# Dilated scores of a two-layer decoder: high and low parts in place of plain fp32, two heads in the two row halves

## The reference, cut to what matters

```python
cq, ck, cv, rq, rk, rv, rg = jnp.split(h @ w_in, cuts, axis=-1)
q = rotary(cq, pos, ROPE_DIM, ROPE_THETA); k = rotary(ck, pos, ROPE_DIM, ROPE_THETA)
scores = jnp.einsum('brnqhd,brnkhd->brnhqk', qs, kk) * (dh ** -0.5)   # per window and dilation
p = jnp.exp(scores - m)                                               # softmax per row
```

## Time and profile before

| | before |
|---|---|
| median of 3 runs | 1432.67 us (1432.28 to 1432.73) |
| profiled execution, its own time | 1432.46 us |
| its span in the trace | 1430.7 us |
| PE busy | 1420.2 us, 99% |
| DVE / ACT / POOL busy | 728.8 / 532.8 / 107.5 us |
| granted TensorE clock | 0.998 of full speed |
| PE's share of the chain that ended last | 96% |

### The profile page before, as it was taken

The page is one execution under the profiler, slowest core; times in us unless marked ns, Lnnn a source line. Parts: engine busy times, 40 slices in busy tenths (PEclk is TensorE's granted clock), DMA queues, the critical chain, the costliest instruction groups (busy, mean ns, idle before and its releaser), DMA issues.

```text
span 1430.7 us, 17936 instructions
## 1 busy us (share of the span) xinstructions
PE 1420.2 (99%) x6780; PEld 1181.7 (83%) x6780; DVE 728.8 (51%) x1025; ACT 532.8 (37%) x809; POOL 107.5 (8%) x90
## 2 busy tenths in 40 slices
PE   9999999999999999999999999999999999999998
PEld 8888888888888888888877788988888888888887
DVE  6656655454444443334567755765544444443332
ACT  5632544332323222322645634543433222322221
POOL 0012200200000000100201111100020000000010
PEclk9999999999999999999999999999999999999999
DMA  8721321232232333333321112541133232233321
GB/s 333 259 88 60 118 74 45 90 101 91 100 102 89 103 100 107 103 104 133 99 78 53 66 45 75 191 141 65 59 103 103 89 102 91 100 101 104 99 78 60
DMA packets 41514, 146.73 MB, mean 103 GB/s; under 512 B 4976, under 2 KB 5104, under 8 KB 41456
## 3 DMA queue, kind: packets, MB, share of 16 engines
q1 hardware_dynamic: 38288, 138.17, 28.9%
q10 hardware_dynamic: 3168, 7.74, 1.5%
HBM read 143.79 MB, written 2.10 MB: 102 GB/s over the span
## 4 chain that ended last, share of the span: by engine, by line
PE 96%; DVE 1%; ACT 1%; issue 1%; DMA 0%; SPq 0%; POOLq 0%; POOL 0%; ACTq 0%
PE acc L1436 28%; PE acc L1438 28%; PE acc L1437 28%; PE acc L1484 3%; PE acc L1486 3%; PE acc L1485 3%; PE aux L1779 1%; PE acc L1803 1%; PE aux L1791 1%; DMA raw<-in_weights 0%; PE aux L1438 0%; PE aux L1437 0%; PE aux L1436 0%; DVE xpt_lo L1143 0%; DVE xp L1160 0%
## 5 line engine op out<-in xcount | busy, mean ns | idle before, releaser
L879 DVE TENSOR_TENSOR w_lo<-raw,w_hi 128x1024 fp32r<-128x1024 f32 x255 | 314.7, 1235 | 328.5 <-ACT w_hi L444 328.4
L1436 PE MATMUL acc<-u_hi,w_hi 128*128 128x512 f32 x1056 | 413.0, 391 | 0.0
L1438 PE MATMUL acc<-u_hi,w_lo 128*128 128x512 f32 x1056 | 411.1, 389 | 0.0
L1437 PE MATMUL acc<-u_lo,w_hi 128*128 128x512 f32 x1056 | 410.9, 389 | 0.0
L444 ACT ACTIVATE w_hi<-raw 128x1024 fp32r<-128x1024 f32 x255 | 268.1, 1052 | 375.9 <-DVE tmp L1235 192.2
L1436 PEld LDWEIGHTS acc<-u_hi,w_hi 128*128 128x128 f32 x1056 | 198.3, 188 | 42.4 <-issue 2.3
L1438 PEld LDWEIGHTS acc<-u_hi,w_lo 128*128 128x128 f32 x1056 | 198.2, 188 | 41.7
L1437 PEld LDWEIGHTS acc<-u_lo,w_hi 128*128 128x128 f32 x1056 | 198.3, 188 | 40.4
L1436 PE MATMUL acc<-act_hi,w_hi 128*128 128x512 f32 (+1 forms) x374 | 141.6, 379 | 0.0
L1438 PE MATMUL acc<-act_hi,w_lo 128*128 128x512 f32 (+1 forms) x374 | 140.9, 377 | 0.0
L1437 PE MATMUL acc<-act_lo,w_hi 128*128 128x512 f32 (+1 forms) x374 | 140.8, 377 | 0.0
(11 more groups left out here) (195 smaller groups left out, 1598.1 us busy)
## 6 DMA issues: line engine op xcount, KB each, us to landing
raw<-in_weights SPq DMA_DIRECT2D x255, 512.0 KB, 3.5
hT<-in_x_t ACTq DMA_DIRECT2D x4, 512.0 KB, 6.4
x_tok<-in_x ACTq DMA_DIRECT2D x4, 512.0 KB, 6.8
out_h<-y_tok SPq DMA_DIRECT2D x4, 512.0 KB, 2.7
mem_tok<-in_mem SPq DMA_DIRECT2D x1, 1024.0 KB, 9.1
memT<-in_mem_t SPq DMA_DIRECT2D x3, 256.0 KB, 5.3
raw<-in_weights SPq DMA_DIRECT2D x2, 256.0 KB, 4.6
cs_d<-in_cs_d ACTq DMA_DIRECT2D x1, 512.0 KB, 3.5
```

The costliest lines, as they stand in the source:

```text
L879: dve.tensor_tensor(w_lo[:, s, :], raw[:, s, :], w_hi[:, s, :].bitcast(F32), ALU.subtract)\
L1436: pe.matmul(out, w_h, x_h, start=first, stop=False)
L1437: pe.matmul(out, w_h, x_l, start=False, stop=False)
L1438: return pe.matmul(out, w_l, x_h, start=False, stop=last)
```

## The change

Rotated q and k of the dilated heads go to a ring of three tiles (`turned_d`). ScalarE rounds each to fp32r (`dil_hi_part`) and VectorE subtracts (`dil_lo_part`). The scores become three matmuls of these parts for each block of rows, and each of the three is issued for the one head and then for the other. A block of `scores` is now rows (0, 1) or (2, 3) of both heads, where it was all rows of one head. `rotate` and `partners` of the dilated tiles stand one unit further back. In the loop over pairs VectorE's `masked`, `maxima` and `normalise` are spread differently.

```diff
-        tq_d = at("tq_d", 8, [P, 4, S])
-        tk_d = at("tk_d", 24, [P, 4, S])
+        tq_hi = at("tq_hi", 8, [P, 4, S], F32R)
+        tq_lo = at("tq_lo", 0, [P, 4, S], F32R)
+        tk_hi = at("tk_hi", 24, [P, 4, S], F32R)
+        tk_lo = at("tk_lo", 16, [P, 4, S], F32R)
+        turned_d = at("turned_d", 82, [P, 3, S])
...
+        def rot_tile(r):
+            return turned_d[:, r % 3, :] if r < 8 else tq[:, r - 8, :]
+        def dil_parts(r):
+            return (tq_hi, tq_lo) if r < 4 else (tk_hi, tk_lo)
+        def ds_tile(p, i, e):
+            return aux_at["ds", p] + 2 * i + e
...
+                def dil_hi_part(r):
+                    act.wait_ge(rot_ready, r + 1)
+                    act.activation(dil_parts(r)[0][:, r % 4, :], turned_d[:, r % 3, :], ACT.Copy).then_inc(dhi_ready, 1)
...
-                    partners(j, a0 + B_QK + j, 32)
+                    if j:
+                        partners(j - 1, a0 + B_QK + j - 1, 32)
+                    if j >= 3:
+                        dil_hi_part(j - 3)
                 for n in range(4):
                     split(u0 + U_RV + n + LEAD)
+                    if n == 0:
+                        partners(7, a0 + B_QK + 7, 32)
+                        dil_hi_part(5)
+                    if n == 1:
+                        dil_hi_part(6)
+                        dil_hi_part(7)
                     if n in (1, 2):
                         exps(n - 1)
...
                 def rotate(r):
-                    dst = (tq_d if r < 4 else tk_d)[:, r % 4, :] if r < 8 else tq[:, r - 8, :]
+                    dst = rot_tile(r)
+                    if 3 <= r < 8:
+                        dve.wait_ge(dlo_ready, r - 2)
                     cs = cs_d if r < 8 else cs_r
                     dve.tensor_tensor(dst, tmp[:, r % 2, :], cs[:, 0, :], ALU.mult)
                     dve.wait_ge(shifted, r + 1)
                     dve.tensor_tensor(tmp[:, 2 + r % 2, :], tmp[:, 2 + r % 2, :], cs[:, 1, :], ALU.mult)\
                         .then_inc(rot_half, 1)
-                def masked(p, heads):
-                    for e in heads:
-                        for i in range(TT):
+                def dil_lo_part(r):
+                    dve.wait_ge(dhi_ready, r + 1)
+                    hi, lo = dil_parts(r)
+                    dve.tensor_tensor(lo[:, r % 4, :], turned_d[:, r % 3, :], hi[:, r % 4, :].bitcast(F32), ALU.subtract)\
+                        .then_inc(dlo_ready, 1)
+                def masked(p, rows):
+                    for i in rows:
+                        for e in range(2):
                             o, w = ROWS[i]
-                            t = aux_at["ds", p] + 4 * e + i
+                            t = ds_tile(p, i, e)
                             dve.wait_ge(aux_done, t + 1)
                             dve.scalar_tensor_tensor(out=dp[:, e, o:o + w], in0=auxs[t % 4][:, 0:w],
                                                      scalar=float(DH) ** -0.5, in1=band[:, S - w:S], op0=ALU.mult,
                                                      op1=ALU.add).then_inc(aux_free_v, 1)
+                def maxima(p, e):
...
                     if j >= 2:
+                        rotate(j - 2)
                         dve.wait_ge(rot_half, j - 1)
                     scaled(a0 + B_QK + j, tmp[:, j % 2, :])
-                    if j:
-                        rotate(j - 1)
+                    if j >= 4:
+                        dil_lo_part(j - 4)
                 for n in range(4):
                     split(u0 + U_RV + n + LEAD)
                     if n == 0:
+                        dil_lo_part(4)
+                        rotate(6)
+                    if n == 1:
                         rotate(7)
-                    if n == 1:
+                        dil_lo_part(5)
                         dve.wait_ge(rot_half, 8)
-                        masked(0, (0, 1))
-                        maxima(0)
+                        masked(0, range(TT))
+                        maxima(0, 0)
+                        maxima(0, 1)
                     if n >= 2:
+                        dil_lo_part(4 + n)
                         normalise(n - 2)
...
                     side(first)
                     if p + 1 < DIL_H // 2:
-                        masked(p + 1, (0,))
+                        masked(p + 1, (0, 1))
                     side_rotate(first)
+                    if p + 1 < DIL_H // 2:
+                        masked(p + 1, (2, 3))
+                        maxima(p + 1, 0)
                     y_lo_part(p, acc(t)[:, :], PHM1 + p + 1, acc_drained)
                     if p + 1 < DIL_H // 2:
-                        masked(p + 1, (1,))
-                        maxima(p + 1)
+                        maxima(p + 1, 1)
                     side(second)
+                    if p + 1 < DIL_H // 2:
+                        normalise(2 * p + 2)
                     side_rotate(second)
                     if p + 1 < DIL_H // 2:
-                        normalise(2 * p + 2)
                         normalise(2 * p + 3)
...
-                def scores(p, e):
-                    pe.wait_ge(rot_ready, 5 + p)
-                    q = slice(DH * e, DH * (e + 1))
-                    for i in range(TT):
-                        t = aux_at["ds", p] + 4 * e + i
-                        aux_free(pe, t)
-                        pe.matmul(auxs[t % 4][:, 0:(i + 1) * P], tq_d[q, p, i * P:(i + 1) * P],
-                                  tk_d[q, p, 0:(i + 1) * P], start=True, stop=True).then_inc(aux_done, 1)
+                def scores(p, rows):
+                    pe.wait_ge(dlo_ready, 5 + p)
+                    for i in rows:
+                        tok, keys = slice(i * P, (i + 1) * P), slice(0, (i + 1) * P)
+                        outs = [auxs[ds_tile(p, i, e) % 4][:, keys] for e in range(2)]
+                        q = [slice(DH * e, DH * (e + 1)) for e in range(2)]
+                        for e in range(2):
+                            aux_free(pe, ds_tile(p, i, e))
+                        for e in range(2):
+                            pe.matmul(outs[e], tq_hi[q[e], p, tok], tk_hi[q[e], p, keys], start=True, stop=False)
+                        for e in range(2):
+                            pe.matmul(outs[e], tq_lo[q[e], p, tok], tk_hi[q[e], p, keys], start=False, stop=False)
+                        for e in range(2):
+                            pe.matmul(outs[e], tq_hi[q[e], p, tok], tk_lo[q[e], p, keys], start=False, stop=True)\
+                                .then_inc(aux_done, 1)
...
-                           after=lambda q: scores(0, q) if q < 2 else None)
+                           after=lambda q: scores(0, (2 * q, 2 * q + 1)) if q < 2 else None)
...
-                        scores(p + 1, 0)
+                        scores(p + 1, (0, 1))
                     values(p)
                     if p + 1 < DIL_H // 2:
-                        scores(p + 1, 1)
+                        scores(p + 1, (2, 3))
```

More of the change, by code:

```diff
@@ L303, in program @@
         rot_ready = sem("rot_ready")
+        dhi_ready = sem("dhi_ready")
+        dlo_ready = sem("dlo_ready")
         dve_step = sem("dve_step")
@@ L1266, in masked @@
                                                      op1=ALU.add).then_inc(aux_free_v, 1)
-                def maxima(p):
-                    for e in range(2):
-                        for i in range(TT):
[L1272 to L1275, removed]
+                def maxima(p, e):
+                    for i in range(TT):
+                        o, w = ROWS[i]
+                        dve.wait_ge(aux_free_v, freed_v(ds_tile(p, i, e)))
+                        dve.tensor_reduce(nmax[:, e, i:i + 1], dp[:, e, o:o + w], AX.X, ALU.max,
+                                          negate=True).then_inc(max_ready, 1)
                 def normalise(h):
```

## The result

The changed kernel takes 1424.32 us (median of four runs, 1424.19 to 1424.54) where the kernel before took 1432.55 beside it: a ratio of 0.9942 (0.993 to 0.9954), 8.2 us or 0.57% faster. The forecast was 1424.7. The profiled execution took 1424.38 us with a span of 1422.6.

What follows compares the result with a forecast made beforehand. TensorE bounds the kernel, busy 1420.2 of 1430.7 us. Streams save 9.5 us, less waits of 0.4 and 1.2, so 7.9 off 1432.46 gives 1424.6, plus 0.2 for the median: 1424.7 us, range 1422.8 to 1430.9.

Steps and rivals of the forecast that it cites:

- The streams: TensorE's score blocks: each of four pairs of heads falls from 4.26 to 1.88 us, 9.5 us saved.
- 1.88, 2.64 and 3.76 us for a pair: TensorE's score matmuls per pair: halves side by side 1.88 (taken), weight loads queueing 2.64, single file 3.76 us.
- 128 columns: Score matmuls of 128 columns in fp32r: 0.109 us each, taken from the transposes; upper bound 0.21, costing 1.2 us more.
- The first block's new wait: First score block waits for tile 4's low part, expected 2.2 us ahead of TensorE: no wait.
- Behind the retention values: After head 0's transposes, TensorE waits once for VectorE's drain of the retention values to free an acc tile: 0.4 us.
- At the transposes of heads 3 and 5: TensorE waits for an aux tile at the transitions to pairs 1 and 2: 0.6 us more each, 1.2 together.
- The sum: Whole kernel: 9.5 less 0.4 less 1.2 gives 7.9 us saved, forecast 1424.7 us.
- (a): Rival on score blocks: weight loads of the two halves queue, a pair takes 2.64 us, 1427.4 us; chance 0.17.
- (b): Rival on score blocks: the halves run in single file, no change that can be told, 1431.1 us; chance 0.14.
- (c): Rival on score blocks: each change of half is a mode change costing 0.19 us, 1448.9 us, slower; chance 0.05.
- (d): Rival: the halves run together and VectorE has room, so neither wait appears, 1423.1 us; chance 0.05.
- (e): Rival: halves run together, but the chains behind are later, 2 to 4 us more, 1426.7 to 1428.7; chance 0.06.

Runs made afterwards that it cites:

- halves without parts: Kernel before the change with only the two heads of a pair issued alternately into the two row halves, in plain fp32: 1424.40 us, ratio 0.9941.
- parts without halves: Changed kernel, but a block of scores is again one head with all four rows, still in high and low fp32r parts: 1430.53 us, ratio 0.9984.
- three then three: Changed kernel, but inside each block of rows one head's three products are issued before the other's three: 1424.32 us, ratio 0.9944.
- six-then-six kernel: Changed kernel, but a block issues head 0's six matmuls before head 1's six, and VectorE takes results once all are done: 1429.96 us, ratio 0.9982.
- the kernel that normalises first: Changed kernel with both heads' exponentials ahead of the second side unit's partners, and both normalisations ahead of its rotation: 1423.41 us.

## Why the prediction was right

By its own steps, in the order of the sum:

- **The streams: 9.5 us forecast.** Eight blocks were 18.8 us and are 9.25 (four each of 0.88 to 0.89 and of 1.42 to 1.43): 9.55 us. The choice between 1.88, 2.64 and 3.76 us for a pair was the whole question, and 1.88 was right: a pair's two blocks are 2.31 us, which is 1.88 and 0.43 for entering and leaving both. That the halves cause it, and nothing else in the change, is shown by both one-sided kernels: halves without parts give all of the gain, parts without halves 2.1 us. The forecast block lengths of 1.1 and 1.7 us count both edges; so counted, the first block is 724.05 - 717.50 - 5.45 = 1.10.
- **128 columns.** 0.11 us, as taken from the transposes. The upper bound of 0.21 does not occur.
- **The first block's new wait: none forecast.** None appeared; the low part of tile 4 ends 2.2 us ahead, as worked out.
- **Behind the retention values: 0.4 us forecast, 0.26 measured.** Against the second block of scores TensorE came 0.95 us earlier (1.0 forecast) and VectorE's drain 0.5 us later, at 12.8 us where before it was at 12.3 (0.7 forecast). Moving two subtractions out of the chain removed the wait. It takes both: the parts without the halves and the halves without the parts have none. The trace itself names no releaser for that half unit, which the forecast had expected to see.
- **At the transposes of heads 3 and 5: 0.6 us more each forecast, 0.56 measured.** The size was right, and head 3's transposes last 2.0 us as forecast (764.07 to 766.07). Of the chain given for it, the scaling of the second unit came with no idle before it, as worked out. Counted from the second block of the pair's scores, VectorE was ready for it at 7.85 us (755.59 - 747.74) where before it was at 7.43 (758.68, the end of its split, less 751.25), and TensorE was done 0.92 us sooner: 0.42 + 0.92 - 0.77 of idle is 0.57. What I had not seen is that ScalarE's exponentials were only the nearer of two limits: with them out of the way VectorE held it, lengthened by GpSimd's add. In the changed kernel that add (758.95 to 760.24) fell into VectorE's idle time of 1.07 us, in which it waited for ScalarE, and cost nothing.
- **The sum.** 9.55 - 0.26 - 1.11 = 8.2 us by the trace, and the spans differ by 8.1 (1430.7 and 1422.6); forecast 7.9. All three terms were off by 0.14 us or less and in the same direction, so no error hid another.

Rivals (a), (b) and (c) are out by the trace: pairs of loads and of matmuls start together and no step stands between halves. (d) and (e) are out by the two waits, which came, and at about the forecast size. One thing behind the forecast was never tested by it: I took alternate issue to be what pairs the halves. It isn't needed. Three matmuls of one half in a row, then three of the other, do as well.

The Trainium skill ("TensorE: Matmul & The Clock Gate", Part 3, what overlaps) has matmuls start and end strictly in program order. By that rule three then three would have been an estimated 1427.9 us, and that was my theory. The traces differ: it measured 1424.32, and in the six-then-six kernel the seventh matmul started ahead of the fourth. The measurement decides: across row halves the order of starts isn't the order of issue.

## What to carry to other kernels

Where a contraction has only 64 rows and two independent ones exist, put them into different row halves and issue them near each other: it nearly halved the time of the eight blocks here, for plain fp32 (18.8 to 10.2 us) as for the parts (16.9 to 9.3), and that plain form needs no extra work on other engines. Splitting into high and low parts brought only another 1 us of stream, and its gain was first eaten by waits. After such a gain, look at once for what has come too late by about as much, and read the idle time in brackets of the engine ahead in that chain: 0.77 us of idle before the scaling was the whole reserve, against 0.92 us that TensorE gained and 0.42 that VectorE's path grew by.

## What the hardware showed that I had not expected

- Matmuls for one row half start ahead of those queued for the other, but not from any distance: with two waiting in front the other half's first started at once (three then three), with five in front it started only when three were left (six then six, 0.28 us late). Where exactly the limit lies, in matmuls or in queued instructions, wasn't tried further.
- VectorE and GpSimd hold each other until the one that started first is done: a normalisation took 2.31 us for 1.28 beside an add of 1.28 that had started 0.04 us before it, and the add took 2.21 us for 1.28 when it started 0.16 us behind a split. Whichever started first kept its length. Not every operation is held: in the kernel that normalises first, the scaling at 761.21, which reads PSUM, kept its 0.68 us beside the running add, and the multiply behind it, with both operands in SBUF, took 1.18 for 0.68. This is what the Trainium skill ("SBUF — State Buffer", "Who interferes with whom") says of a port pair that the two engines lock for whole instructions; the rows agree. The hold was already in the kernel before the change. It cost nothing there, because ScalarE's exponentials, which the next normalisation needs, ended no sooner than the held one (763.77 and 763.78). VectorE's timeline there:

```profile
761.46 2.32 DVE L1283 TENSOR_SCALAR dp<-dp,pinv 128x128 f32<-128x128 f32 x4
...
764.01 1.27 DVE L1283 TENSOR_SCALAR dp<-dp,pinv 128x128 f32<-128x128 f32 x4
```
